# Two adjacent rows of w_down on each partition: an expert's second weight matrix in rows of 8 KB, and transposes that read every second column

## The chip, the cores and the metric

The kernel runs on one core of a Trainium2 chip. The metric is the device time of one execution in microseconds (us). Smaller is better. TensorE is called PE below, its weight loads PEld, VectorE DVE, ScalarE ACT, GpSimd POOL and the engine that issues most transfers SP.

## What is computed

One decoder layer on 512 prompt tokens and 32 sample tokens of width 1024: a mixer, then a mixture of 32 experts of which each token uses four, then a gated embedding and a last norm. The change lies in the experts. Cut to that part, the reference is:

```python
def expert_block(args):
    xe, e = args                                   # 128 rows that use expert e
    gu = xe @ w_up[e] + b_up[e]                    # 128x1024 @ 1024x2048
    glu = jnp.minimum(gu[:, :D_FF], SWIGLU_LIMIT)
    lin = jnp.clip(gu[:, D_FF:], -SWIGLU_LIMIT, SWIGLU_LIMIT)
    act = glu * jax.nn.sigmoid(SWIGLU_ALPHA * glu) * (lin + 1.0)
    return act @ w_down[e] + b_down[e]             # 128x1024 @ 1024x1024
```

The inner dimension of `act @ w_down[e]` has 1024 members. They may be summed in any grouping, if the column of `act` and the row of `w_down[e]` that meet are the same one.

## The kernel before

The kernel begins with the mixer and the router. Then it goes through the experts, one block of up to 128 gathered tokens for each. The weights of an expert come from HBM in twelve chunks of 1 MB: eight of `w_up` (128 rows of 2048 numbers, one row on each partition) and four of `w_down`. A chunk of `w_down` holds 256 rows of 1024 numbers. Before the change, partition p gets row p of the first 128 (`j = 0`) and row p of the second 128 (`j = 1`), so its 8 KB come from two places in HBM, 4 KB each. All chunks go through one ring of six buffers, `raw` (`RING = 6`). SP issues a load as soon as the buffer it needs is free, which is when DVE has read the chunk that came six before it (`raw_free`, which waits on `s_lo`).

The matrix products are made of numbers that are split into a high part, rounded to the type fp32r, and a rest. For each chunk ACT copies `raw` into `w_hi` (line 937), DVE subtracts and writes `w_lo` (line 1865), and PE makes three products: the high and the low part of the activations with `w_hi` (`hi_products`, line 1401, eight matmuls of 512 columns), and the high part with `w_lo` (`lo_products`, line 1410, four matmuls). In each the activations are the stationary operand, loaded by an LDWEIGHTS, and the weights stream past.

The order on each engine is written out by hand. In the PE's `step(J)`, eight up-chunks of the next block run with the down-chunks of block J behind them:

- `up_start` puts the bias into PSUM (line 1418, four matmuls).
- After the second up-chunk comes `a_transposes(J)` (line 1389). It transposes the activation of block J, `lin`, in eight pieces of 128x128 into the PSUM region `tp`. In a piece the columns of `lin` are the stationary operand (one LDWEIGHTS of 128 columns), and the identity matrix streams past. In the profile such a row reads `ps<-ident,lin`.
- ACT then copies `tp` to `aT_hi` (`aT_high`, line 958) and DVE makes `aT_lo` of it (`aT_low`, line 1946). These two are the stationary operands of the down-products: in chunk c and half j, `dn_args` takes piece `2c+j` of them with the columns `j*D` to `j*D+D` of the chunk.
- After the first down-chunk comes `x_transposes(J + 2)` (line 1382), the same for the gathered rows `x_rows` of a later block.

There are 32 blocks (no expert has a second block of tokens here), so `a_transposes` runs 32 times: 31 times in `step` and once behind it, for the last block. SP's `step` issues the eight loads `load_up` and then the four loads `load_dn` of each block. POOL gathers the rows of a block and scatters its results by indirect transfers.

After the last block come the gate weights (four chunks whose layout the change leaves as it is), the sum of each token's four expert rows, and the outputs.

Of the kernel before, what the change touches and what calls it, by code (L numbers as in the profile page):

```python
# [30 lines left out]
P = 128  # L31
RING = 6
SPLIT = 3
UP_CHUNKS = 8
DN_CHUNKS = 4
# [5 lines left out]
def build(nc, x_prompt, x_sample, state_pool, p_prompt, p_sample, norm_mix, w_in, w_pool, pool_scale,  # L41
# [31 lines left out]
    xn_dram = nc.dram_tensor("xn_rows", [T, D], F32, kind="Internal").ap()  # L73
    y4_dram = nc.dram_tensor("expert_rows", [T * TOPK, D], F32, kind="Internal").ap()
    up_dram = w_up.rearrange("a e (c p) n -> (a e c) p n", p=P)
    dn_dram = w_down.rearrange("a e (c j p) n -> (a e c) p j n", p=P, j=2)

    ctx = ExitStack()
    with ctx:
        def sb(name, shape, dt=F32, scope=ctx):  # L80
            return scope.enter_context(nc.sbuf_tensor(name, shape, dt))

        def sem(name):
            return ctx.enter_context(nc.semaphore(name))


        ident = sb("ident", [P, P])
# [69 lines left out]
        with ExitStack() as s:  # L157
            raw = sb("raw", [P, RING, 2 * FF], scope=s)
# [100 lines left out]
        with ExitStack() as s:  # L259
            w_hi = sb("w_hi", [P, SPLIT, 2 * FF], F32R, scope=s)  # L260
            w_lo = sb("w_lo", [P, SPLIT, 2 * FF], F32R, scope=s)
            lin = sb("lin", [P, FF], scope=s)
# [74 lines left out]
        def slot(s):  # L337
            return (s + 2) % RING
# [58 lines left out]
        ring = [sem(f"raw_landed_{i}") for i in range(RING)]  # L397
# [89 lines left out]
        tp = ps[:, 6:8, :].rearrange("p a b -> p (a b)")  # L487
# [35 lines left out]
        def _(sp):  # L523
# [42 lines left out]
            def raw_free(J, s):  # L566

                if isinstance(J, int):

                    if s < 2:  # L570
                        sp.wait_ge(s_outa, 1)
                    else:
                        sp.wait_ge(s_outp, TT)
                    if STEP_CHUNKS * J + s >= RING:
                        wait_lo(sp, J, s - RING)
                    return
                lo = sp.to_reg(J * STEP_CHUNKS + (s - RING + 1))
                sp.wait_ge(s_lo, lo)
# [5 lines left out]

            def load_dn(J, s, e, c):
                raw_free(J, s)
                sp.dma_start(raw[:, slot(s), :].rearrange("p (j n) -> p j n", j=2),
                             dn_dram[bass.ds(e * DN_CHUNKS + c, 1), :, :, :].rearrange(
                                 "a p j n -> p (a j) n")).then_inc(ring[s % RING], 16)

            def step(J, e_up, e_dn):
                for c in range(UP_CHUNKS):
                    load_up(J, UP_CHUNKS + c, e_up, c)
                for c in range(DN_CHUNKS):
                    load_dn(J, 2 * UP_CHUNKS + c, e_dn, c)
# [30 lines left out]
            for c in range(DN_CHUNKS):  # L626
                load_dn(n_over + (E - 1), UP_CHUNKS + c, e_dn, c)
# [455 lines left out]
        def _(pe):  # L1083
# [246 lines left out]
            for t in range(LAST):  # L1330
                for k in range(KP):
                    mm = pe.transpose(ps[:, k, t * P:(t + 1) * P], p_sb[:, t, k * P:(k + 1) * P], ident[:])
            mm.then_inc(s_pTp, 1)
            h2_transposes(LAST)
            for k in range(KP):
                mm = pe.transpose(ps[:, 3, k * NS:(k + 1) * NS], p_sb[0:NS, LAST, k * P:(k + 1) * P], ident[0:NS, 0:NS])
# [15 lines left out]
            for t in range(TT):  # L1352
                mm = pe.matmul(count_cols, ones_r[0:NT[t], :], mask[0:NT[t], t, :], start=(t == 0), stop=(t == LAST))
# [31 lines left out]
            def a_transposes(u):  # L1385
                pe.wait_ge(s_act, u + 1)
                pe.wait_ge(s_xlo, u + 2)
                for k in range(KD):
                    mm = pe.transpose(tp[:, k * P:(k + 1) * P], lin[:, k * P:(k + 1) * P], ident[:])  # L1389
                mm.then_inc(s_atp, 1)  # L1390

            def hi_products(J, s, out, parts, fresh=False, late_low=0):
# [61 lines left out]
            def step(J, first=False, over=False):  # L1454
                up_start(J + 1, late_low=first)
                for c in range(UP_CHUNKS):
                    up_hi(J, UP_CHUNKS + c, c, late_low=J + 2 if first and c == 0 else 0)
                    if c > 0:
                        up_lo(J, UP_CHUNKS + c - 1, c - 1)
                    elif not first:  # L1460
                        dn_lo(J, UP_CHUNKS - 1, DN_CHUNKS - 1)
                    if c == 1:
                        a_transposes(J)
                    if c == 5 and over:
                        over_slots()
                for c in range(DN_CHUNKS):
                    if c == 0:
                        if first:
                            pe.wait_ge(s_ple0d, 2)
                        if over:  # L1470
                            pe.wait_ge(s_overd, 1)
                        dn_start(J)
                    dn_hi(J, 2 * UP_CHUNKS + c, c)
                    if c > 0:
                        dn_lo(J, 2 * UP_CHUNKS + c - 1, c - 1)
                    else:
                        up_lo(J, 2 * UP_CHUNKS - 1, UP_CHUNKS - 1)
                        x_transposes(J + 2)
# [29 lines left out]
            with pe.If(n_over > 0):  # L1508
                with pe.Fori(0, OVER) as b:
                    with pe.If(b < n_over):  # L1510
                        step(b + (E - 1))
            J = n_over + (E - 1)
            a_transposes(J)
            dn_lo(J, UP_CHUNKS - 1, DN_CHUNKS - 1)

# [44 lines left out]
            def gate_products(i, x, rows, b, w, start=False, stop=False):  # L1560
                for k in range(KD):
                    cols = slice(b * 512, (b + 1) * 512)
                    mm = pe.matmul(gate_bank(i)[0:rows, b, :], x[:, i % 2, k, 0:rows],  # L1563
                                   gate_hi[k // 2][:, k % 2, cols] if w == "hi" else gate_lo[:, k, cols],
                                   start=(start and k == 0), stop=(stop and k == KD - 1), skip_group_check=True)
                return mm
# [12 lines left out]
            for i in range(1, TT):  # L1579
# [11 lines left out]
                if i < LAST:  # L1591
                    x2_transposes(i + 1)
                    pe.wait_ge(s_x2l, i + 1)
                    for b in range(2):
                        mm = gate_products(i, x2T_lo, P, b, "hi", stop=True)
# [591 lines left out]
```

## Time and profile before

| | before |
|---|---|
| median of 3 runs | 1425.4 us |
| lowest and highest run | 1425.33 and 1426.13 us |
| span of the profiled execution (first to last instruction) | 1423.6 us |
| the profiled execution's own time | not listed apart from the three runs; its span is 1.8 us below their median |
| mean granted clock of PE, in parts of full speed | 0.991 |
| busy share of PE, PEld, DVE, ACT, POOL | 98%, 81%, 88%, 66%, 15% |
| moved by DMA | 457.35 MB in 94171 packets |

The span leaves out what lies around the first and the last instruction. The busy share of PE is made of matmuls that overlap each other, so 98% says that there was nearly always one under way, not that PE ran at its peak. The slices of the page (40 of about 35.6 us each) show in tenths how busy an engine was. By chance one slice is nearly as long as one block of an expert.

### The profile page before, as it was taken

To read this page: it belongs to the slowest core of one execution; us is meant where nothing else is said; L and a number is where in the kernel's file an instruction comes from. 1 tells how busy PE (TensorE), PEld (TensorE's weight loads), DVE (VectorE), ACT (ScalarE), POOL (GpSimd) and SP (SyncE) were. 2 spreads that over 40 slices of the span, in tenths; PEclk is the share of its full clock that TensorE was granted. 3 is DMA by queue.
4 is the path that set the end of the run, shared out by engine and by line. 5 is a ranking of instruction groups with operands and counts; after the bars stand their busy time and mean duration, and the time that the engine had idled before them with its cause. 6 is when DMAs were issued, how large, how long until landed. Compare 5 with 4: busy or idle time off the path is not lost.

```text
span 1423.6 us, 19576 instructions
## 1 busy us (share of the span) xinstructions
PE 1392.7 (98%) x6631; PEld 1146.6 (81%) x6631; DVE 1255.5 (88%) x1030; ACT 934.6 (66%) x634; POOL 216.8 (15%) x130
## 2 busy tenths in 40 slices
PE   7999999999999999999999999999999999999997
PEld 5898777888888888888888888888888888888665
DVE  5866488999999999999999999999999999999885
ACT  4313157777777777777777777777777777777522
POOL 3141000131111111111111111111111111111100
PEclk9999989999999999999999999999999999999998
DMA  7113487999999999999999999999999999999561
GB/s 264 60 63 117 149 300 295 373 354 371 372 374 369 371 374 370 370 370 368 370 368 368 371 368 374 371 371 374 375 373 374 371 371 374 367 375 361 198 233 59
DMA packets 94171, 457.35 MB, mean 321 GB/s; under 512 B 13314, under 2 KB 14894, under 8 KB 60213
## 3 DMA queue, kind: packets, MB, share of 16 engines
q1 hardware_dynamic: 84255, 437.50, 80.9%
q0 software_dynamic: 9360, 17.85, 3.3%
q10 hardware_dynamic: 526, 1.60, 0.5%
q8 instruction: 19, 0.31, 0.1%
q14 instruction: 11, 0.09, 0.0%
HBM read 451.76 MB, written 21.58 MB: 332 GB/s over the span
## 4 chain that ended last, share of the span: by engine, by line
PE 82%; DVE 1%; issue 1%; DMA 1%; ACT 1%; POOLq 0%; POOL 0%; DVEq 0%; ACTq 0%
PE ps L1401 49%; PE ps L1410 24%; PE ps L1563 2%; PE ps L1382 2%; PE ps L1389 2%; PE ps L1418 2%; DVE resid L2093 1%; DMA x_rows<-xn_rows,token_of 0%; PE ps L1556 0%; DMA expert_rows<-y_rows,scatter_col 0%; DMA raw<-expert_rows 0%; PE ps L1342 0%; ACT w_hi L937 0%; PE ps L1371 0%; DVE w_lo L1865 0%
## 5 line engine op out<-in xcount | busy, mean ns | idle before, releaser
L1865 DVE TENSOR_TENSOR w_lo<-raw,w_hi 128x2048 fp32r<-128x2048 f32 x384 | 867.8, 2286 | 58.0 <-PE ps L1410 57.5
L937 ACT ACTIVATE w_hi<-raw 128x2048 fp32r<-128x2048 f32 x384 | 732.3, 1916 | 213.4 <-PE ps L1401 174.5
L1401 PE MATMUL ps<-w_hi,xT_hi 128*128 128x512 f32 x1024 | 278.6, 394 | 3.2 <-ACT w_hi L937 2.0
L1401 PE MATMUL ps<-w_hi,xT_lo 128*128 128x512 f32 x1024 | 275.2, 391 | 0.0
L1410 PE MATMUL ps<-w_lo,xT_hi 128*128 128x512 f32 x1024 | 273.8, 389 | 0.0
L1401 PEld LDWEIGHTS ps<-w_hi,xT_lo 128*128 128x128 f32 x1024 | 192.7, 188 | 41.5
L1410 PEld LDWEIGHTS ps<-w_lo,xT_hi 128*128 128x128 f32 x1024 | 192.2, 188 | 40.1
L1401 PEld LDWEIGHTS ps<-w_hi,xT_hi 128*128 128x128 f32 x1024 | 190.0, 188 | 42.0 <-ACT w_hi L937 2.7
L774 POOL DMA_INDIRECT expert_rows<-y_rows,scatter_col x32 | 143.6, 4487 | 404.1 <-ACT y_rows L968 404.1
L1401 PE MATMUL ps<-w_hi,aT_hi 128*128 128x512 f32 x512 | 139.9, 395 | 0.0
L1401 PE MATMUL ps<-w_hi,aT_lo 128*128 128x512 f32 x512 | 136.8, 389 | 0.0
L1410 PE MATMUL ps<-w_lo,aT_hi 128*128 128x512 f32 x512 | 136.7, 389 | 0.0
L766 POOL DMA_INDIRECT x_rows<-xn_rows,gather_col x30 | 30.5, 1016 | 548.8 <-PE ps L1382 515.1
L1401 PEld LDWEIGHTS ps<-w_hi,aT_lo 128*128 128x128 f32 x512 | 96.1, 188 | 20.1
L1410 PEld LDWEIGHTS ps<-w_lo,aT_hi 128*128 128x128 f32 x512 | 96.0, 188 | 19.9
L1401 PEld LDWEIGHTS ps<-w_hi,aT_hi 128*128 128x128 f32 x512 | 93.8, 188 | 17.8
L968 ACT ACTIVATE y_rows<-ps 128x1024 f32<-128x1024 f32 x32 | 32.9, 1028 | 75.9 <-PE ps L1410 75.9
L1951 DVE TENSOR_SCALAR glu<-ps 128x1024 f32<-128x1024 f32 x32 | 39.2, 1224 | 14.7 <-PE ps L1410 14.6
L1946 DVE TENSOR_TENSOR aT_lo<-ps,aT_hi 128x1024 fp32r<-128x1024 f32 x32 | 38.9, 1216 | 1.9 <-ACT aT_hi L958 1.9
L954 ACT ACTIVATE xT_hi<-ps 128x1024 fp32r<-128x1024 f32 x33 | 33.3, 1008 | 10.4 <-PE ps L1410 9.2
L1957 DVE SCALAR_TENSOR_TENSOR lin<-lin,glu 128x1024 f32<-128x1024 f32 x32 | 39.0, 1218 | 0.0
L1941 DVE TENSOR_TENSOR xT_lo<-ps,xT_hi 128x1024 fp32r<-128x1024 f32 x32 | 39.0, 1218 | 0.0
(297 smaller groups left out, 1199.2 us busy)
## 6 DMA issues: line engine op xcount, KB each, us to landing
raw<-in_w_up_dram SPq DMA_DIRECT2D x256, 1024.0 KB, 6.8
raw<-in_w_down_dram SPq DMA_DIRECT2D x128, 1024.0 KB, 7.7
raw<-in_w_ple_gate_dram SPq DMA_DIRECT2D x4, 1024.0 KB, 5.4
yk<-expert_rows SPq DMA_DIRECT2D x4, 1024.0 KB, 7.9
raw<-expert_rows SPq DMA_DIRECT2D x4, 1024.0 KB, 7.0
resid<-in_x_prompt_dram SPq DMA_DIRECT2D x4, 512.0 KB, 7.0
w_v_sb<-in_w_in_dram SPq DMA_DIRECT2D x2, 1024.0 KB, 7.7
w_z_sb<-in_w_in_dram SPq DMA_DIRECT2D x2, 1024.0 KB, 12.5
```

What stands on the lines that cost most here:

```text
L766: pool.indirect_dma_start(x_rows[:], None, xn_dram[:, :], bass.IndirectOffsetOnAxis(ap=col, axis=0), bounds_check=last_token, oob_is_err=F ...
L774: pool.indirect_dma_start(y4_dram[:, :], bass.IndirectOffsetOnAxis(ap=scatter_col[:, 0:1], axis=0), y_rows[:], None, bounds_check=last_row ...
L937: act.activation(w_hi[:, s % SPLIT, :], raw[:, slot(s), :], ACT.Copy).then_inc(s_hi, 1)
L954: act.activation(xT_hi[:].rearrange("p k n -> p (k n)"), tp, ACT.Copy).then_inc(s_xhi, 1)
L968: act.activation(y_rows[:], dn, ACT.Copy).then_inc(s_y, 1)
L1401: mm = pe.matmul(out[:, c:c + 512], (xh, xl)[xs], w_hi[:, s % SPLIT, base + c:base + c + 512], start=(fresh and xs == 0 and base == 0), st ...
L1410: mm = pe.matmul(out[:, c:c + 512], xh, w_lo[:, s % SPLIT, base + c:base + c + 512], start=False, stop=last and k == len(parts) - 1, skip_ ...
L1865: dve.tensor_tensor(w_lo[:, s % SPLIT, :], raw[:, slot(s), :], w_hi[:, s % SPLIT, :].bitcast(F32), ALU.subtract).then_inc(s_lo, 1)
L1941: dve.tensor_tensor(xT_lo[:].rearrange("p k n -> p (k n)"), tp, xT_hi[:].rearrange("p k n -> p (k n)").bitcast(F32), ALU.subtract).then_in ...
L1946: dve.tensor_tensor(aT_lo[:].rearrange("p k n -> p (k n)"), tp, aT_hi[:].rearrange("p k n -> p (k n)").bitcast(F32), ALU.subtract).then_in ...
L1951: dve.tensor_scalar(glu[:], gu[:, 0:FF], LIMIT, None, ALU.min).then_inc(s_glu, 1)
L1957: dve.scalar_tensor_tensor(out=lin[:], in0=lin[:], scalar=1.0, in1=glu[:], op0=ALU.add, op1=ALU.mult).then_inc(s_act, 1)
```

## The change

The view `dn_dram` of `w_down` is cut differently. A chunk still has the same 256 rows, but partition p now gets rows 2p and 2p+1, which lie next to each other in HBM, so its 8 KB are one run. The load is written as 128 rows of 2048 numbers, like that of `w_up`. To match, piece `k = 2c+j` of the transposed activation has to hold the columns `256c + 2i + j` for i from 0 to 127. `a_transposes` therefore takes as its stationary operand every second column of `lin`, beginning at `256c + j`. In memory the 128 numbers of one LDWEIGHTS were 4 bytes apart and are now 8 bytes apart.

```diff
-    dn_dram = w_down.rearrange("a e (c j p) n -> (a e c) p j n", p=P, j=2)
+    dn_dram = w_down.rearrange("a e (c p j) n -> (a e c) p (j n)", p=P, j=2)
...
             def load_dn(J, s, e, c):
                 raw_free(J, s)
-                sp.dma_start(raw[:, slot(s), :].rearrange("p (j n) -> p j n", j=2),
-                             dn_dram[bass.ds(e * DN_CHUNKS + c, 1), :, :, :].rearrange(
-                                 "a p j n -> p (a j) n")).then_inc(ring[s % RING], 16)
+                sp.dma_start(raw[:, slot(s), :], dn_dram[bass.ds(e * DN_CHUNKS + c, 1), :, :].rearrange(
+                    "a p n -> p (a n)")).then_inc(ring[s % RING], 16)
...
             def a_transposes(u):
                 pe.wait_ge(s_act, u + 1)
                 pe.wait_ge(s_xlo, u + 2)
+                rows_of = lin[:].rearrange("p (c i j) -> p c j i", i=P, j=2)
                 for k in range(KD):
-                    mm = pe.transpose(tp[:, k * P:(k + 1) * P], lin[:, k * P:(k + 1) * P], ident[:])
+                    mm = pe.transpose(tp[:, k * P:(k + 1) * P], rows_of[:, k // 2, k % 2, :], ident[:])
                 mm.then_inc(s_atp, 1)
```

Nothing else is edited. No engine gets an instruction more or fewer, none changes its place, and every semaphore and wait stays. The operands `aT_hi` and `aT_lo` and the chunks in `raw` have the same shapes as before.

## Rows read from the trace of the kernel before

**Rows 1.** The page: busy time, and busy tenths in 40 slices of the span.

```profile
PE 1392.7 (98%) x6631; PEld 1146.6 (81%) x6631; DVE 1255.5 (88%) x1030; ACT 934.6 (66%) x634; POOL 216.8 (15%) x130
...
PE   7999999999999999999999999999999999999997
...
DMA  7113487999999999999999999999999999999561
```

**Rows 2.** Stretches by engine: busy us, instructions, granted clock, DMA share, GB/s.

```profile
core 0: us, PE busy (x) PEld busy (x) DVE busy (x) ACT busy (x) POOL busy (x), PEclk, DMA share, GB/s
180.00:230.00 50.00, 44.88 (x183) 34.00 (x183) 39.78 (x56) 28.48 (x21) 3.30 (x3) 0.86 0.74 268
230.00:265.00 35.00, 35.00 (x163) 29.04 (x162) 34.79 (x25) 26.85 (x18) 2.22 (x2) 1.00 0.94 364
800.00:1290.00 490.00, 490.00 (x2269) 407.43 (x2268) 456.55 (x293) 364.47 (x221) 73.63 (x28) 1.00 0.97 371
1342.00:1424.00 82.00, 68.19 (x293) 48.58 (x291) 59.65 (x57) 23.16 (x30) 4.43 (x6) 0.93 0.39 147
```

**Rows 3.** The chain that ended last, pieces: start us, us, what.

```profile
724.35 1.81 PE ps L1401 x8
726.16 0.91 PE ps L1410 x4
727.07 0.87 PE ps L1389 x8
727.94 1.84 PE ps L1401 x8
...
762.47 0.87 PE ps L1389 x8
...
1375.44 10.90 PE ps L1563 x48
```

**Rows 4.** DMA issues: size of one, median us from issue to landing.

```profile
raw<-in_w_up_dram SPq DMA_DIRECT2D x256, 1024.0 KB, 6.8
raw<-in_w_down_dram SPq DMA_DIRECT2D x128, 1024.0 KB, 7.7
```

**Rows 5.** Line 587, loads of w_down: ns min/median/max, and us to landing.

```profile
L587 SPq DMA_DIRECT2D raw<-in_w_down_dram x128: 372/373/388, 231.0 to 1313.3; - x128
DMA to landing us min/median/max: 4.9/7.7/10.0
```

**Rows 6.** Readers and writers of raw: idle before them (us, times) until what.

```profile
its engine sat idle before it (us, times) until:
  PE ps L1401: 174.5, 216
  PE ps L1410: 57.5, 113
  DVE w_lo L1865: 36.2, 35
  DMA xn_rows<-xn: 2.7, 1
  ACT w_hi L937: 0.3, 1
  DMA raw<-expert_rows: 0.2, 1
```

**Rows 7.** PE's loads by form: busy us, mean ns, idle before.

```profile
L1389 PEld LDWEIGHTS ps<-ident,lin 128*128 128x128 f32 x256 | 29.9, 141 | 5.7 <-issue 1.7
L1184 PEld LDWEIGHTS ps<-ident,new_cols 128*32 128x32 f32 x4 | 0.4, 97 | 0.1
L1556 PEld LDWEIGHTS ps<-ident,resid 32*128 32x128 f32 x8 | 0.6, 136 | 2.5 <-DVE resid L2093 2.5
L1401 PEld LDWEIGHTS ps<-w_hi,xT_hi 128*128 128x128 f32 x1024 | 190.0, 188 | 42.0 <-ACT w_hi L937 2.7 <-ACT xT_hi L954 1.4
L1103 PEld LDWEIGHTS ps<-w_v_hi,xTh 128*32 128x32 f32 x8 | 0.9, 109 | 0.9
```

**Rows 8.** PE's loads in order of time, at 77.7 us: start us, us, what.

```profile
77.71 0.43 PEld L1182 LDWEIGHTS ps<-ident,ext 128*15 128x15 f32 x4
78.15 0.42 PEld L1184 LDWEIGHTS ps<-ident,new_cols 128*32 128x32 f32 x4
78.59 0.19 PEld L1194 LDWEIGHTS ps<-diff,w_pool_sb 128*128 128x128 f32 x1
```

**Rows 9.** PE's loads in order of time, at 1355.1 us, transposes of 32 rows.

```profile
1355.11 0.57 PEld L1556 LDWEIGHTS ps<-ident,resid 32*128 32x128 f32 x8 [2.52 <-DVE resid L2093]
```

## Prediction

> **What bounds the kernel now.** I read the page first: PE was busy in 98% of the span, DVE in 88%, and the slices show PE at 9 from the second to the last but one, while the DMA engines, too, stand at 9 through the experts [rows 1]. So two things look full, and the question is which of them sets the time. The stretches answer it. From 800 to 1290 us PE is busy for 490.00 of 490 us at clock 1.00, with DVE at 456.55; already in the first block, from 230 to 265, PE has no gap [rows 2]. The DMA share is 0.97 there, but nothing waits for it: among all that the readers of `raw` waited for, no load of `w_up` or `w_down` appears. They waited for PE (174.5 and 57.5 us) and for each other; the only transfers named are the stores of `xn_rows` (2.7 us, once) and the expert rows of the end (0.2 us) [rows 6]. The chain that ended last shows the same from the other side. It consists of PE's own pieces with no gap, and the period from one `a_transposes` to the next is 762.47 - 727.07 = 35.40 us, of which the eight transposes take 0.87 us, or 109 ns each [rows 3]. Whatever the change does, it costs or gains in the experts what it adds to or takes from PE's instructions, unless it makes PE wait.
>
> **The loads of w_down.** There are 128 of them. Each becomes 128 runs of 8 KB where it was 256 runs of 4 KB; that is 32768 - 16384 = 16384 runs fewer, with the same bytes. What a load of the new form takes is shown by `w_up`, which has it already: 6.8 us to landing against 7.7 us [rows 4]. I expect the loads of `w_down` to land up to 0.9 us sooner. That is worth nothing, and the cover can be given: a load is issued when the buffer is free, six chunks ahead. Six chunks are half a period, 35.40 / 2 = 17.7 us, and the slowest of the 128 landed after 10.0 us [rows 5]. If ACT begins its copy about one chunk (2.95 us) before PE uses it, 17.7 - 2.95 - 10.0 = 4.7 us are left over in the worst case. SP's own issue of 373 ns [rows 5] may shrink too; SP waits for DVE before each load and hands nothing to PE. What queues behind it on SP is the next load, with the same spare time. A lower DMA share lets POOL's gathers and scatters finish sooner; PE has no gap that they end in the blocks. At the end of the program the DMA share is 0.39 [rows 2] and no load of `w_down` is left. Sum of this part: 0.
>
> Could less traffic make PE's matmuls themselves shorter? Twelve matmuls of 512 columns take 1.81 + 0.91 = 2.72 us in the blocks, 227 ns each, with the DMA engines at 0.97; 48 of the end take 10.90 us, also 227 ns each, at a share of 0.39 over that stretch [rows 2, 3]. So no.
>
> **The strided transposes.** Here is the one place where the change touches the path. There are 32 x 8 = 256 of them, 256 x 109 ns = 27.9 us in all. No row shows an LDWEIGHTS of every second column, so I bound it. What sets the 109 ns? Either the load of 128 columns of `lin`, or the pass of 128 columns of the identity. Two rows separate these. Transposes with a load of only 15 or 32 columns but the same pass of 128 follow each other at the same pace: the first four loads begin at 77.71, the next four at 78.15, the one after at 78.59, so 0.44 us for four, 110 ns each [rows 8]. The load is not what sets the pace. And transposes with the full load of 128 columns but a pass of only 32 go faster: eight loads in 0.57 us, the last of them 136 ns long, so (570 - 136) / 7 = 62 ns each [rows 7, 9]. A load therefore occupies 62 ns at most, under a pass of 109 ns, and has **47 ns to spare**.
>
> Now the stride. The part of a load that grows with its columns is (141 - 97) / 96 = 0.46 ns a column, 59 ns for 128 [rows 7]. Low end: every second column costs nothing extra, 0 us. Below nothing there is no room, since the pass of the identity is unchanged. Middle: a column costs twice as long, so a load occupies at most 62 + 59 = 121 ns, and each transpose grows by at most 12 ns: 256 x 12 ns = 3.1 us; if the 62 ns are set by something other than the load, less or nothing. High end: a column costs four times as long, as it would if a fetch brought four neighbours before and each fetch now served a single column; then a load is 62 + 3 x 59 = 239 ns, a transpose grows by 130 ns, and 256 of them by 33.3 us. I take 0. With every second number read, a run of four numbers still serves two columns, and twice the load time is the most that halved density asks for; of that 47 of 59 ns are hidden. It is also the nearest row: the load that I measure is contiguous and hidden by nearly half of its pass.
>
> The Trainium skill ("SBUF — State Buffer", section "Door 1: The DMA port swizzle", its note on cachelines) says that a 16-byte line must be hit at least twice in succession for full bandwidth and that crossing to a new line more often costs. Every second fp32 hits each line exactly twice, so by it the stride is free, at its edge; the stride after this one would not be. No row here has a stride, so the trace neither confirms nor denies it.
>
> The skill's page "TensorE: Matmul & The Clock Gate", section "LDWEIGHTS (loading the stationary operand)", speaks against the change. It prices a load at its columns over 1.2 GHz, which is 107 ns for 128. By that there would be only 2 ns to spare, and twice the load would cost up to 256 x 105 ns = 27 us as an estimate from the page. The rows agree for the fp32r loads of the products, (188 - 109) / 96 = 0.82 ns a column, and disagree for the transposes, which run at 0.46 ns a column and repeat every 62 ns [rows 7, 9]. The measured value decides, so I keep the 47 ns.
>
> **What follows a transpose.** ACT's copy to `aT_hi`, DVE's `aT_lo` and the down-products read the same shapes in the same order. `a_transposes` stands some six chunks ahead of the first down-product, so even 1 us more there delays only PE's own next instruction.
>
> **The sum.** 1423.6 + 0 + 0 = 1423.6 us of span. The median of the runs is 1.8 us above that span and I keep the distance: **1425.4 us**. A measurement of this kernel can tell about 0.2%, or 2.9 us, from no change.
>
> **The rivals.**
>
> - *A line for each column.* Place: the eight LDWEIGHTS of each `a_transposes`. If the stride costs a load more than the 47 ns that are hidden, the rest is paid 256 times, straight on PE. It decides from there: 11 ns past the cover are 2.9 us. At the high end it gives 1425.4 + 33.3 = 1458.7 us; a load that occupies 170 ns would give 256 x 61 ns = 15.6 us, 1441.0 us. For it: no row shows a strided load and PE has no gap to absorb anything. Against it: half of each fetched run is still used. Chance 0.12.
> - *Twice the load, partly covered.* The middle case above: up to 3.1 us, 1428.5 us at most. Since 62 ns is an upper bound, half or more of this case falls within 0.2%. Chance 0.20, of which 0.08 is above 0.2%.
> - *Transfers pay after all.* The freed DMA time would have to end a wait. The only stretch with idle PE near the loads is 180 to 230 us, where 50.00 - 44.88 = 5.1 us are idle at clock 0.86 [rows 2]; `w_down` is first loaded at 231.0 us [rows 5], so it has no part in it. The blocks have no gap. At most the loads' 0.9 us could appear on the last block, and a change of the granted clock in the first blocks or at the end could add a few: 1421 to 1425 us. Chance 0.08 for over 0.2% faster.
> - *The transfer is not what the edit says.* If a run of 8 KB is cut into pieces of 4 KB by whatever makes the packets, landing stays at 7.7 us and the packets do not fall. The time is then the same. It would show in the packets under 8 KB and lies inside the forecast.
>
> **How the numbers follow.** The forecast, load hidden and transfers worth nothing, has 0.60. With the 0.12 of the doubled load that stays within 0.2%, "same" has 0.72; slower is 0.12 + 0.08 = 0.20, faster 0.08. The range has to take in the doubled load, 1428.5 us, and the 0.7 us by which runs lie above their median, so it reaches to 1429.5. Below it takes 2.4 us, of which 0.9 us are the sooner landing and the rest the difference from one execution to another, to 1423.0. Left out are the costly stride and most of the faster case, together some 0.2.
>
> **What would show it.** Right: `a_transposes` at 0.87 us in the chain for eight, a period of 35.40 us, PE busy for 490 of 490 us; loads of `w_down` landing in about 6.8 us; about 16384 packets fewer in total; DMA share a little under 0.97, SP's issue not longer than its 373 ns. The LDWEIGHTS of line 1389 may get longer, up to about 200 ns, without any effect. Wrong: eight transposes that take over 0.97 us in the chain (the period then grows by the same amount), or a period that shrinks, which would mean that PE's pace did hang on the transfers.

## The result and the profile after

The change makes the kernel slower by 3 to 5 us.

| | before | after |
|---|---|---|
| median, runs side by side | 1426.32 us (16 runs) | 1429.48 us (16 runs) |
| lowest and highest run | 1423.82 to 1427.65 us | 1428.16 to 1433.33 us |
| ratio after to before | | 1.0027, 95% interval 1.0020 to 1.0034 |
| span of the profiled execution | 1423.6 us | 1426.4 us |
| that execution's own time | | 1428.16 us |

The ratio makes 0.0027 x 1426.3 = 3.9 us, with an interval of 2.9 to 4.8 us; the medians lie 3.2 us apart. The first place to look is the line of the transposes. Below are its LDWEIGHTS, before and after, with the shortest, median and longest in ns and the start of the first and the last.

Line 1389 of the kernel before:

```profile
L1389 PEld LDWEIGHTS ps<-ident,lin x256: 138/141/146, 228.8 to 1324.5; 128*128 128x128 f32 x128
```

Line 1389 of the kernel after:

```profile
L1389 PEld LDWEIGHTS ps<-ident,lin x256: 196/209/220, 227.2 to 1326.8; 128*128 128x128 f32 x128
```

By the medians a load of every second column takes 209 ns instead of 141, 68 ns more. From the first load to the last there are 31 blocks. They took 1324.5 - 228.8 = 1095.7 us before and take 1326.8 - 227.2 = 1099.6 us now. This difference of 3.9 us accounts for the result (that it meets the ratio to the tenth is chance, as single executions scatter by 2 us and more). The profiled spans differ by only 2.8 us, mainly because this execution ran for longer at the full clock ahead of the blocks, as the stretches of the kernel after show (same columns as in [rows 2]):

```profile
180.00:230.00 50.00, 43.84 (x193) 33.74 (x193) 41.39 (x58) 29.92 (x22) 3.31 (x3) 0.93 0.74 278
230.00:265.00 35.00, 35.00 (x163) 29.16 (x162) 34.73 (x24) 26.74 (x18) 3.74 (x2) 1.00 0.94 366
800.00:1290.00 490.00, 490.00 (x2262) 407.69 (x2261) 455.43 (x292) 364.55 (x222) 73.75 (x28) 1.00 0.96 370
1342.00:1424.00 82.00, 70.58 (x301) 50.02 (x299) 62.14 (x58) 24.68 (x32) 4.44 (x6) 0.96 0.40 147
```

From 180 to 230 us the granted clock was 0.93 against 0.86 in [rows 2], and the first load came 1.6 us earlier. The first strided transposes and the first load of `w_down` come only at 227 and 229 us, so the change has no part in this stretch. In the blocks PE still has no gap: 490.00 of 490 us, now with 2262 matmuls instead of 2269.

The chain that ended last, kernel after (start us, us, what), shows where a block became longer:

```profile
727.29 0.95 PE ps L1389 x8
728.24 1.85 PE ps L1401 x8
730.09 0.92 PE ps L1410 x4
...
747.33 0.88 PE ps L1381 x8
748.21 1.85 PE ps L1401 x8
750.05 0.92 PE ps L1410 x4
...
762.82 0.95 PE ps L1389 x8
```

Against [rows 3], the eight transposes of `lin` take 0.95 instead of 0.87 us, 119 instead of 109 ns each, and the period is 762.82 - 727.29 = 35.53 instead of 35.40 us. Of these 0.13 us the transposes explain 0.08. The rest, some 0.05 us, lies for the most part in the product groups behind both kinds of transposes, each 0.01 to 0.02 us longer. Those behind `x_transposes` (line 1381 now, an unchanged instruction) took 1.83 and 0.91 us before:

```profile
747.01 0.87 PE ps L1382 x8
747.89 1.83 PE ps L1401 x8
749.72 0.91 PE ps L1410 x4
```

The transfers did what the edit says. DMA issues and the loads of `w_down` in the kernel after:

```profile
DMA packets 77787, 457.35 MB, mean 321 GB/s; under 512 B 13314, under 2 KB 14894, under 8 KB 27445
...
raw<-in_w_up_dram SPq DMA_DIRECT2D x256, 1024.0 KB, 6.6
raw<-in_w_down_dram SPq DMA_DIRECT2D x128, 1024.0 KB, 7.3
```

```profile
L587 SPq DMA_DIRECT2D raw<-in_w_down_dram x128: 332/333/347, 229.3 to 1315.7; - x128
DMA to landing us min/median/max: 4.8/7.3/9.6
```

There are 94171 - 77787 = 16384 packets fewer, exactly. A load of `w_down` lands after 7.3 instead of 7.7 us, and SP spends 333 instead of 373 ns on it [rows 4, 5]. As PE has no gap in the blocks, none of this could shorten them.

### The profile page after: what moved, and what is told of

It is laid out like the page before. It is cut to its first block, busy times and chain, and to the rows that moved or that the text cites. A ratio compares the mean times of both kernels' runs of the same rounds, so it can differ in the third digit from the quotient of the medians.

```text
span 1426.4 us, 19576 instructions
## 1 busy us (share of the span) xinstructions
PE 1394.7 (98%) x6631; PEld 1149.4 (81%) x6631; DVE 1256.7 (88%) x1030; ACT 935.0 (66%) x634; POOL 216.0 (15%) x130
## 2 busy tenths in 40 slices
DMA packets 77787, 457.35 MB, mean 321 GB/s; under 512 B 13314, under 2 KB 14894, under 8 KB 27445
## 4 chain that ended last, share of the span: by engine, by line
PE 82%; DVE 1%; issue 1%; DMA 1%; ACT 1%; POOLq 0%; POOL 0%; DVEq 0%; ACTq 0%
PE ps L1401 49%; PE ps L1410 24%; PE ps L1563 2%; PE ps L1389 2%; PE ps L1381 2%; PE ps L1418 2%; DVE resid L2093 1%; DMA x_rows<-xn_rows,token_of 0%; PE ps L1556 0%; DMA expert_rows<-y_rows,scatter_col 0%; PE ps L1341 0%; DMA raw<-expert_rows 0%; ACT w_hi L936 0%; PE ps L1370 0%; DVE w_lo L1865 0%
## 5 line engine op out<-in xcount | busy, mean ns | idle before, releaser
L1951 DVE TENSOR_SCALAR glu<-ps 128x1024 f32<-128x1024 f32 x32 | 39.2, 1224 | 13.7 <-PE ps L1410 13.7
```

Of the source, the lines that this page charges most:

```text
L1951: dve.tensor_scalar(glu[:], gu[:, 0:FF], LIMIT, None, ALU.min).then_inc(s_glu, 1)
```

## The experiments

Periods below are taken from PE's matmuls in order of time: the eight transposes of `lin` begin once in each block, and the difference of two starts is the period. For the kernel before it is 762.31 - 726.91 = 35.40 us, and for the kernel after:

```profile
727.13 1.11 PE L1389 MATMUL ps<-ident,lin 128*128 128x128 f32 x8
762.66 1.11 PE L1389 MATMUL ps<-ident,lin 128*128 128x128 f32 x8
798.20 1.11 PE L1389 MATMUL ps<-ident,lin 128*128 128x128 f32 x8
```

From the third on, the periods of one execution agree to about 0.01 us, with one exception: one block holds 20 matmuls more (line 1371) and takes 37.67 us in the kernel before. So periods tell far more than times do. Each run below has them from one profiled execution.

### One half of the change at a time

The stride alone, on the kernel before:

```diff
-                    mm = pe.transpose(tp[:, k * P:(k + 1) * P], lin[:, k * P:(k + 1) * P], ident[:])
+                    mm = pe.transpose(tp[:, k * P:(k + 1) * P], rows_of[:, k // 2, k % 2, :], ident[:])
```

> Only the transposes change (every second column of lin); the loads of w_down stay at two runs of 4 KB, so the down-product pairs columns and rows that do not belong together. Theory 'the stride costs': all of the +3 to 4 us stays, ratio to before 1.002 to 1.003; LDWEIGHTS of line 1389 at 206 to 209 ns, eight transposes 0.95 us in the chain, period 35.53 us. Rival 'part of it comes from the 8 KB loads': the transposes account for 32 x 0.08 = 2.6 us alone, ratio about 1.0018, period 35.48 us.

Measured: 1429.73 us median against 1427.01 us, ratio 1.0025 (1.0015 to 1.0034).

```profile
727.69 1.11 PE L1390 MATMUL ps<-ident,lin 128*128 128x128 f32 x8
763.22 1.11 PE L1390 MATMUL ps<-ident,lin 128*128 128x128 f32 x8
```

The period is 35.53 us and the load lasts 206 ns on average, as in the whole change. The longer product groups are there too: 1.85 and 0.92 us behind `x_transposes`. So they do not come from the new loads.

The layout alone, on the kernel after:

```diff
-                    mm = pe.transpose(tp[:, k * P:(k + 1) * P], rows_of[:, k // 2, k % 2, :], ident[:])
+                    mm = pe.transpose(tp[:, k * P:(k + 1) * P], lin[:, k * P:(k + 1) * P], ident[:])
```

> Only the loads of w_down change (one run of 8 KB a partition); the transposes read contiguous columns as before, so the down-product pairs columns and rows that do not belong together. Theory 'the stride costs all': ratio 1.000, period 35.40 us, LDWEIGHTS 141 ns. Rival 'part of it comes from the 8 KB loads': period 35.45 us, ratio about 1.0009, with matmuls that are slower behind both kinds of transposes. Theory 'the loads pay': ratio below 0.999.

Measured: 1427.19 us against 1427.01 us, ratio 1.0003 (0.9994 to 1.0012).

```profile
728.83 1.03 PE L1388 MATMUL ps<-ident,lin 128*128 128x128 f32 x8
764.23 1.03 PE L1388 MATMUL ps<-ident,lin 128*128 128x128 f32 x8
```

The period is 35.40 us, to the last digit that of the kernel before. The transfers of 8 KB neither gain nor cost that could be seen. The stride is the whole cause of the slowdown.

### The same layout without a stride on PE

DVE's two clamps (lines 1951 and 1952) read every second column of PSUM and write `glu` and `lin` in sorted order, so the transposes are contiguous and the new loads stay:

```diff
-                dve.tensor_scalar(glu[:], gu[:, 0:FF], LIMIT, None, ALU.min).then_inc(s_glu, 1)
+                dve.tensor_scalar(by_row(glu[:]), every_second(gu[:, 0:FF]), LIMIT, None, ALU.min).then_inc(s_glu, 1)
...
+            def every_second(x):
+                return x.rearrange("p (c i j) -> p c j i", i=P, j=2)
+            def by_row(x):
+                return x.rearrange("p (c j i) -> p c j i", i=P, j=2)
```

(`lin` likewise.)

> Full computation. New loads; DVE's two clamps read every second column of PSUM and write glu and lin sorted, so that the transposes are contiguous again. If a strided read costs DVE nothing: clamps at 1.22 us, period 35.40 us, ratio to before 1.000. If DVE's strided PSUM read costs twice the time (2 x 1.2 us a block more), DVE's 2.4 us of spare time a block are used up and PE begins to wait for w_lo: period 35.4 to 36 us, ratio 1.000 to 1.017.

Groups by line on DVE (busy us, mean ns, idle before), first in the kernel before:

```profile
L1951 DVE TENSOR_SCALAR glu<-ps 128x1024 f32<-128x1024 f32 x32 | 39.2, 1224 | 14.7 <-PE ps L1410 14.6
L1952 DVE TENSOR_SCALAR lin<-ps 128x1024 f32<-128x1024 f32 x32 | 38.8, 1212 | 0.0
```

and with the sorting clamps:

```profile
L1956 DVE TENSOR_SCALAR glu<-ps 128x1024 f32<-128x1024 f32 x32 | 39.2, 1224 | 13.4 <-PE ps L1409 13.3
L1957 DVE TENSOR_SCALAR lin<-ps 128x1024 f32<-128x1024 f32 x32 | 38.9, 1215 | 0.0
```

The clamp that writes `glu` takes 1224 ns on average in both, the one that writes `lin` 1215 instead of 1212 ns. In these two instructions DVE reads fp32 from PSUM at a stride of 8 bytes for nothing. The period is 761.32 - 725.92 = 35.40 us. The times were less clear: median 1427.49 us, but 2 of 12 executions at 1442 us, ratio 1.0023 (0.9997 to 1.0048). So the same kernel ran again:

> The kernel with the sorted clamps once more, unchanged (new loads, DVE's clamps sort, contiguous transposes), because 2 of its 12 executions lay at 1442 us and none of the kernel before did. If these belong to the kernel, again one or two in ten lie 15 us above the rest; if they were chance, all lie between 1424 and 1432 us and the ratio is 1.000.

Measured: a period of 35.40 us again, 1427.55 us against 1426.19 us, ratio 1.0006 (0.9997 to 1.0015), and none of 11 executions above 1428.44 us. The two outliers did not come back. This is the way to have the rows of 8 KB for nothing. Its period beats that of the kernel after by 0.13 us, and its time is level with the kernel before. One of the twelve executions of the next kernel lay at 1444.81 us too; where these rare executions come from stays open.

### How much does a larger stride cost?

On the kernel after, every fourth column:

```diff
-                rows_of = lin[:].rearrange("p (c i j) -> p c j i", i=P, j=2)
+                rows_of = lin[:].rearrange("p (c i j) -> p c j i", i=P, j=4)
```

with `rows_of[:, k // 4, k % 4, :]`.

> As the change, but the transposes take every fourth column (16 bytes apart), so the down-product pairs columns and rows that do not belong together. Theory 'a fetch brings two neighbours (8 bytes) and both strides use one of them': as the change, LDWEIGHTS about 209 ns, period 35.53 us, ratio 1.0027. Rival 'a fetch brings four neighbours (16 bytes) and each fetch costs the same': the load doubles again, LDWEIGHTS near 209 + 118 = 327 ns, a transpose at 239 ns, 256 x 130 ns = 33 us, ratio about 1.023.

Measured: 1430.2 us against 1427.01 us, ratio 1.0036 (1.0018 to 1.0054); the execution at 1444.81 us is part of this ratio, and the medians alone make 1.0022. The loads by form:

```profile
L1389 PEld LDWEIGHTS ps<-ident,lin 128*128 128x128 f32 x256 | 36.0, 209 | 3.7 <-issue 1.5
```

and the period, 763.49 - 727.97 = 35.52 us:

```profile
727.97 1.12 PE L1389 MATMUL ps<-ident,lin 128*128 128x128 f32 x8
763.49 1.12 PE L1389 MATMUL ps<-ident,lin 128*128 128x128 f32 x8
```

A load lasts 209 ns on average against 206 in the kernel after; twice the distance costs almost nothing more. The period is even 0.01 to 0.02 us shorter than that of the kernel after, although the eight transposes take 0.01 us longer. So it is not a price for each 16 bytes that are crossed. By the note on cachelines of the Trainium skill ("SBUF — State Buffer", section "Door 1: The DMA port swizzle"), on which the prediction leaned, two hits on a 16-byte line give full bandwidth, so that every second fp32 would still be free. These loads do not bear that out: the step lies between contiguous (141 ns) and every second column (206 ns), and not behind it.

Is it a price for each column, or one for the load? The same kernel, in which the four transposes of `new_cols` also read every fourth column:

```diff
-                mm = pe.transpose(... new_cols[:, g, :], ident[:])
+                mm = pe.transpose(... new_cols[:].rearrange("p g n -> p (g n)").rearrange("p (n g) -> p g n", g=G)[:, g, :], ident[:])
```

> As the run with stride 4, and besides the four transposes of new_cols (32 columns each, line 1184 of the kernel before) read every fourth column too; new_pool_sample is then made of the wrong columns. It asks whether a stride costs per column or per load. Per column: 128 columns cost 209 - 141 = 68 ns more, so 32 columns cost 17 ns more, 97 + 17 = 114 ns. Per load: 97 + 68 = 165 ns. Time and period as with stride 4, 35.51 us.

One execution took 1429.69 us, beside one of the kernel before at 1427.48 us. The loads of `new_cols`:

```profile
L1183 PEld LDWEIGHTS ps<-ident,new_cols x4: 107/107/108, 78.4 to 78.7; 128*32 128x32 f32 x4
```

It is 107 ns, 10 more than the 97 of [rows 7], nearer to the 114 of a price for each column than to the 165 of a price for the load. The price grows with the columns, though not quite in proportion: 10 ns for 32, 68 ns for 128. The slope between these two is now (209 - 107) / 96 = 1.06 ns a column, where contiguous columns had 0.46.

And does it matter where the contiguous columns begin? On the kernel before, one column late:

```diff
-                    mm = pe.transpose(tp[:, k * P:(k + 1) * P], lin[:, k * P:(k + 1) * P], ident[:])
+                    mm = pe.transpose(... lin[:, k * P + (1 if k < KD - 1 else -1):(k + 1) * P + (1 if k < KD - 1 else -1)], ident[:])
```

> The kernel before, but the transposes of lin read 128 contiguous columns that begin one column late (4 bytes off an 8-byte boundary; the last piece one early), so their columns are not those that the product needs. Theory 'two neighbours are had at once, wherever the pair begins': 141 ns, 35.40 us. Rival 'pairs must lie on an 8-byte boundary': LDWEIGHTS about 206 ns and period 35.53 us, as with a stride.

```profile
L1389 PEld LDWEIGHTS ps<-ident,lin 128*128 128x128 f32 x256 | 29.8, 140 | 5.9 <-issue 1.9
```

The load stays at 140 ns; one execution took 1428.09 us, where eight of the kernel before took 1424.06 to 1428.03 us. The period was 764.87 - 729.46 = 35.41 us, 0.01 us longer, without any stride. An odd beginning keeps the fast rate, so what is lost with a stride is not an alignment to 8 bytes.

### Elsewhere on PE

The stride moved to the other transposes, `x_transposes`, with those of `lin` contiguous:

```diff
-                    mm = pe.transpose(tp[:, k * P:(k + 1) * P], x_rows[:, k * P:(k + 1) * P], ident[:])
+                    mm = pe.transpose(... x_rows[:].rearrange("p (c i j) -> p c j i", i=P, j=2)[:, k // 2, k % 2, :], ident[:])
```

> The kernel before, but x_transposes (264 transposes of gathered rows) read every second column and a_transposes stay contiguous; the up-product then pairs columns and rows that do not belong together. Theory 'a strided load of fp32 columns takes twice as long wherever it stands': LDWEIGHTS of line 1382 goes from 141 to about 206 ns, that of lin stays at 141 ns, period 35.40 + 0.09 to 0.14 = 35.49 to 35.54 us. Rival 'something about lin or its place': period 35.40 us.

```profile
L1382 PEld LDWEIGHTS ps<-ident,x_rows 128*128 128x128 f32 x264 | 36.7, 206 | 3.9 <-issue 1.3
L1389 PEld LDWEIGHTS ps<-ident,lin 128*128 128x128 f32 x256 | 29.8, 141 | 5.7 <-issue 1.6
```

One execution, 1429.62 us against a median of 1426.47; period 764.47 - 728.94 = 35.53 us. The stride costs the same in either place. Then both edits together, so that both kinds of transposes are strided:

> The kernel before with both kinds of transposes reading every second column (products pair columns and rows that do not belong together). If the costs add: period 35.40 + 0.19 to 0.27 us = 35.59 to 35.67 us, time to before +6 to +9 us, ratio 1.004 to 1.006. If the extra time behind x_transposes that the change showed (the four product groups there, some 0.03 us a block) was already the same effect, it is counted once and the period is near 35.62 us.

Measured: 1433.13 us against 1426.47 us, ratio 1.0046 (1.0031 to 1.0062), period:

```profile
730.01 1.11 PE L1389 MATMUL ps<-ident,lin 128*128 128x128 f32 x8
765.62 1.11 PE L1389 MATMUL ps<-ident,lin 128*128 128x128 f32 x8
```

765.62 - 730.01 = 35.61 us, 0.21 more than before. Twice the 0.08 of a row of transposes makes 0.16, and the remaining 0.05 is there once, not twice. So the rest does not add up with the number of strided loads.

The products themselves with a strided stationary operand, fp32r, 48 loads a block:

```diff
-                return dn, [(aT_hi[:, 2 * c + j, :], aT_lo[:, 2 * c + j, :], j * D, D) for j in range(2)]
+                cols = [t[:, 2 * c:2 * c + 2, :].rearrange("p a n -> p (a n)").rearrange("p (i j) -> p j i", j=2) for t in (aT_hi, aT_lo)]
+                return dn, [(cols[0][:, j, :], cols[1][:, j, :], j * D, D) for j in range(2)]
```

> The kernel before, but the down-products take every second column of aT_hi and aT_lo (fp32r) as their stationary operand (48 loads a block), so that rows of the result are sorted wrongly. Theory 'an fp32r load already spends on each column what a strided fp32 load does': LDWEIGHTS stays at 188 ns and the period at 35.40 us. Rival 'a stride doubles any load': LDWEIGHTS of ps<-w_hi,aT_hi at 188 + 79 to 188 + 105 ns = 267 to 293 ns; 2 x 105 = 210 ns would then still lie under a pass of 227 ns or just cost a few ns each.

The loads by form, one line of the kernel before and two of this one (busy us, mean ns, idle before them):

```profile
L1401 PEld LDWEIGHTS ps<-w_hi,aT_lo 128*128 128x128 f32 x512 | 96.1, 188 | 20.1
```

```profile
L1401 PEld LDWEIGHTS ps<-w_hi,aT_lo 128*128 128x128 f32 x512 | 98.9, 193 | 20.6
L1410 PEld LDWEIGHTS ps<-w_lo,aT_hi 128*128 128x128 f32 x512 | 98.8, 193 | 20.3
```

The load grows by 5 ns only, from 188 to 193, so nothing is doubled. But the period was 766.48 - 730.77 = 35.71 us: 0.31 us for 48 matmuls, 6.5 ns each, and the one execution took 1435.48 us, against a median of 1426.47. The theory was wrong about the period, and the rival, which allowed for a few ns each, about the load. The product's chain shows it, eight matmuls in 1.87 instead of 1.81 us:

```profile
718.90 1.87 PE ps L1401 x8
720.77 0.93 PE ps L1410 x4
```

So 227 ns are not the pass of 512 columns alone: the pace moved with the stationary operand. The rows of PEld show how. Before, 20.1 us / 512 = 39 ns lie idle between two loads, and 188 + 39 = 227 ns; in this run it is 20.6 us / 512 = 40 ns, and 193 + 40 = 233 ns. What makes the 39 ns no run tells.

### Does a longer pass hide the load?

The explanation so far is that the strided load takes about 119 ns and has only the 109 ns of the pass before it to lie under. Then it should vanish under a product. In two kernels the eight transposes stand one behind each of the eight high products of the third up-chunk (in the 31 blocks of `step`), first with the loads and contiguous transposes of before, then with those of the change. The transposes thus end one chunk later than before, in both:

```diff
                             mm = pe.matmul(out[:, c:c + 512], (xh, xl)[xs], w_hi[:, s % SPLIT, base + c:base + c + 512], ...)
+                            if between is not None:
+                                ...
+                                piece = a_piece(between)
+                                between += 1
...
-                    if c == 1:
-                        a_transposes(J)
```

> Full computation, loads of w_down as before, contiguous transposes. In the 31 blocks of step() the eight transposes no longer stand in a row: one goes behind each of the eight high products of the third up-chunk. It is the yardstick for the next run. If a transpose costs its own pass wherever it stands: period 35.40 us. If each change between product and transpose costs as at the ends of a row (7 to 100 ns), the period grows by up to 0.1 us or more: 35.4 to 36.0 us.

> Full computation, the change's loads and its transposes of every second column, one behind each high product of the third up-chunk. Theory 'the strided load of about 120 ns is exposed only because it has no more than the 109 ns pass of the transpose before it to lie under': under a product of 213 to 227 ns it disappears, so the period equals that of the run with contiguous transposes in the same places within 0.02 us. Rival 'a strided load costs PE its extra time wherever it stands': the period is 0.08 to 0.13 us longer than in that run, 31 x that = 2.5 to 4 us.

Measured, against 1426.19 us: 1429.01 us, ratio 1.0019 (1.0010 to 1.0028), with contiguous columns, and 1430.61 us, ratio 1.0029 (1.0019 to 1.0040), with the stride. The periods, from the matmuls of `x_transposes`, contiguous:

```profile
712.96 1.03 PE L1382 MATMUL ps<-ident,x_rows 128*128 128x128 f32 x8
783.99 1.03 PE L1382 MATMUL ps<-ident,x_rows 128*128 128x128 f32 x8
```

and strided:

```profile
712.57 1.03 PE L1381 MATMUL ps<-ident,x_rows 128*128 128x128 f32 x8
783.64 1.03 PE L1381 MATMUL ps<-ident,x_rows 128*128 128x128 f32 x8
```

Between the two rows lie two blocks: 71.03 / 2 = 35.52 us and 71.07 / 2 = 35.54 us. Under a product the stride costs 0.02 us a block instead of 0.13, although its load still lasts about 200 ns:

```profile
L1393 PEld LDWEIGHTS ps<-ident,lin x248: 196/198/206, 228.3 to 1299.0; 128*128 128x128 f32 x124
```

What the stride adds is thus a matter of cover, for the 0.08 us in the transposes at least. Yet alternating is no gain, since it costs 0.11 us a block by itself.

The run with contiguous transposes shows one thing more. Its chain around `x_transposes`, which this edit leaves alone, reads:

```profile
748.63 0.87 PE ps L1382 x8
749.51 1.85 PE ps L1404 x8
751.35 0.92 PE ps L1422 x4
```

These are the 1.85 and 0.92 us of the kernel after, and neither kind of transposes has a stride in this kernel. So the longer groups behind the unchanged transposes need no stride; the place of the other eight transposes among the products brings them too.

## Why the prediction was wrong

**What bounds the kernel** was right: PE alone, without a gap. The blocks became longer by 0.13 us each in its own instructions, with PE busy for 490.00 of 490 us as before.

**The loads of w_down** were right: worth nothing, and the run with the layout alone shows it at 1.0003, with a period of 35.40 us. The landing fell by 0.4 us, inside "up to 0.9", but to 7.3 us and not to the "about 6.8". The 16384 packets and SP's shorter issue came as said.

**The strided transposes** hold the step that failed: "I take 0". Of the cases with 0, 3.1 and 33.3 us the middle one came true: a load of 62 + 59 = 121 ns was given as the most that a doubled cost a column makes, against a pass of 109, and the transposes now follow each other every 119 ns, so that they cost 0.08 x 32 = 2.6 us instead of nothing. That the two numbers meet so well is in part luck. By the medians of its own length the load grew by 68 ns and not by 59, and the transpose by 10 to 11, so that some 57 ns of the growth were hidden and not 47; the two errors cancel. The choice among the cases was made by an argument without a row ("a run of four numbers still serves two columns") and by the note of the Trainium skill on cachelines, which agreed with it. The rows held a hint to the contrary. [rows 7] showed two rates of a load, 0.46 ns a column for the fp32 transposes and 0.82 for the fp32r products; the fast one is nearly two columns in the time of one. If it is had by taking two neighbours at once, a stride can lose it. Every second and every fourth column then cost alike, which the run with stride 4 shows, and the fp32r loads, which have no fast rate to lose, hardly grow, which the run with strided products shows (188 to 193 ns). The slope of 1.06 ns a column is more than the twice 0.46 that pairing alone would give. That the mechanism is this pairing is an inference; what is measured is the rates, and that the step from contiguous to strided costs while the next one does not.

**"At most 12 ns a transpose, 3.1 us"** was then too small by a term that had no place in the sum. The transposes gave 2.6 us, less than that most. The products around them gave another 0.05 us a block, 1.5 us. I had written that what follows a transpose reads the same shapes in the same order, and put it at nothing. The runs show that the change brings this rest by its stride (it is in the run with the stride alone and not in that with the layout alone), that it appears also behind the unchanged transposes, and that it is there once with both strided. But they also show that a stride is not needed for it: transposes between products bring the same 1.85 and 0.92 us behind `x_transposes` with every load contiguous, and contiguous columns from an odd start bring 0.01 us. Its cause stays open. The run with strided products shows that PE's matmuls of 512 columns are not spaced by their pass alone, but I have no run that shows why a change in one row of transposes alters the products behind the other, twenty microseconds later.

**The rivals.** "Twice the load, partly covered" was the right one, with a chance of 0.20, and only 0.08 of it above 0.2%, because 62 ns was taken for a loose upper bound. It may well have been loose, as some 57 ns were hidden, but the load also grew by more than the 59 ns. "A line for each column" would have cost up to 33 us and is refuted by stride 4, where the period is 35.52 us. The measured 1429.48 us lies at the very edge of the range that ended at 1429.5, on the side to which less than a quarter of the chance was given.

**The 107 ns of the Trainium skill** ("TensorE: Matmul & The Clock Gate", section "LDWEIGHTS (loading the stationary operand)") were set aside for the contiguous transposes, and rightly: by the estimate from them, with 2 ns to spare and a load of twice 107, the cost would have been some 27 us, and 2.6 were measured. For the strided ones that rate, 0.83 ns a column, is nearer than the 0.46 of the contiguous ones, but the measured 1.06 is above it.

## What to carry to other kernels

On an engine without gaps, price a changed access pattern even where the instruction count stays the same, and ask first which fast rate the contiguous form enjoys: here a stride in the stationary operand of an fp32 transpose more than doubled what a load takes for each column (0.46 to 1.06 ns, with every fourth), and with a pass of 109 ns to lie under, 11 of its 68 ns more came through. Put a needed permutation where there is spare time and the pattern is free; DVE's clamps took it at no cost. And larger runs in HBM were worth nothing to this kernel, in which PE has no gap that the loads could fill, although the DMA engines were busy for 0.97 of the time in its blocks.

## What the runs showed of the hardware

- An LDWEIGHTS of 128 fp32 columns for a transpose: 141 ns contiguous, 206 ns with every second, 209 ns with every fourth column (means), and 140 ns when contiguous from an odd column. Slopes 0.46 and, with every fourth, 1.06 ns a column. Unexpected was that stride 2 costs as much as stride 4.
- The same stride on fp32r loads of the products adds 5 ns (188 to 193), and yet the matmuls of 512 columns with such loads then follow each other every 233 instead of 227 ns. I had taken these 227 ns for the matmul's own. In both kernels the pace is the load's length plus 39 or 40 ns.
- Transposes between products cost more than the same ones in a row: 31 blocks at 35.52 instead of 35.40 us, for eight of them. Some 0.03 us of this lies in the products behind the other transposes.
- DVE's clamps read PSUM in fp32 at a stride of 8 bytes at the contiguous speed: 1224 ns for 128x1024 in both (1212 and 1215 ns for the second clamp).
- Blocks of one kernel repeat within 0.01 us, while single executions of the kernel before lie between 1423.82 and 1427.65 us. A period shows an effect of 0.01 us, a time does not. Part of the scatter is the granted clock: in the run with the layout alone it was 0.80 and 0.77 from 312 to 316 and from 316 to 320 us, where it was 1.00 in the kernel before, and that one block took 39.29 instead of 37.67 us.
